# HGRN2 and dilated-window decoder layer with PEER experts: the first half of the tokens multiplied as plain fp32, with whole weight blocks on chip

## The reference, cut to what matters

```python
mod = jax.nn.silu(c) @ w_ada + b_ada                     # 6 x 1024: shifts, scales, gates
n1 = RMSNorm(x) * (1 + sc1) + sh1
h  = n1 @ w_in                                           # 1024 -> 8704: q|f|i|g, q|k|v, two gates
ya = hgrn(h) @ w_branch_a                                # gated linear recurrence, 4 heads of 128
yb = dilated_window_attention(h) @ w_branch_b            # 3 groups of 4 heads; QK norm, partial rotary
x  = x + g1 * ((sigmoid(gl_a) * ya + sigmoid(gl_b) * yb) @ w_out)
n2 = RMSNorm(x) * (1 + sc2) + sh2
q  = rms_norm(n2 @ peer_wq)                              # 8 heads of 256
# top 16 of two times 128 keys, top 16 of their sums, then for each token 128 experts:
x  = x + g2 * sum_k softmax(score)_k * gelu(n2 . u[e_k]) * v[e_k]
```

## Time and profile before

| | us |
|---|---|
| Median of three runs | 4424.8 (4424.0 to 4430.3) |
| Span of the profiled execution | 4435.7 |
| Opening | 0 to 61.4 |
| Projection | 61.4 to 397.3 |
| HGRN | 397.3 to 521.4 |
| Attention, merge | 521.4 to 671.7 |
| Branches | 671.7 to 740.0 |
| Output and second norm | 740.0 to 801.7 |
| Queries, the first gather at 896.3 | 801.7 to 1045.8 |
| Second half beside the experts, and the rest | 1045.8 to 4435.7 |

### The profile page before, as it was taken

How to read it: one execution, slowest core, us unless ns; L and a number is a source line. 1 busy time by engine, 2 the same in 40 slices (tenths; PEclk the granted TensorE clock), 3 DMA queues, 4 the chain that set the end, 5 groups by cost and what they waited for, 6 DMA issues and landing times. The chain is left out here.

```text
span 4435.7 us, 46775 instructions
## 1 busy us (share of the span) xinstructions
PE 3251.9 (73%) x14243; PEld 1706.6 (38%) x14243; DVE 2593.4 (58%) x6557; ACT 1955.8 (44%) x6710; POOL 1472.8 (33%) x1175
## 2 busy tenths in 40 slices
PE   6998868874999999786754687985555555555556
PEld 4677754642543346444432454651111111111111
DVE  2362334476557745584646536656766766766774
ACT  2122431145457734483532225544545545545554
POOL 4543102352322233231212112223444444444443
PEclk8998889986999999787976898987867677777769
DMA  6533244389999999796999978889999999999998
GB/s 258 198 138 129 71 154 171 115 347 356 393 384 356 378 365 387 288 358 232 402 315 383 369 277 308 348 321 383 421 404 421 420 404 415 413 403 414 415 407 334
DMA packets 313374, 1447.75 MB, mean 326 GB/s; under 512 B 42913, under 2 KB 104257, under 8 KB 164770
## 3 DMA queue, kind: packets, MB, share of 16 engines
q0 software_dynamic: 152064, 1107.36, 62.4%
q1 hardware_dynamic: 146690, 330.19, 21.0%
q10 hardware_dynamic: 14368, 7.21, 0.6%
HBM read 1377.25 MB, written 74.57 MB: 327 GB/s over the span
## 5 line engine op out<-in xcount | busy, mean ns | idle before, releaser
L2928 POOL DMA_INDIRECT uv_ring<-in_peer_uv,pick_idx x1024 | 1134.5, 1108 | 2255.1 <-PE expert_acc L3089 1929.2
L3089 PE MATMUL expert_acc<-uv_ring,diag 128*64 128x512 f32 x3968 | 1263.8, 773 | 665.6 <-ACT diag L3059 629.4
L3016 DVE SCALAR_TENSOR_TENSOR uv_ring<-uv_ring,n_pairs 128x1024 f32<-128x1024 f32 x1024 | 1246.5, 1230 | 672.9 <-DMA uv_ring<-in_peer_uv,pick_idx 639.9
L3089 PEld LDWEIGHTS expert_acc<-uv_ring,diag 128*64 128x64 f32 x3968 | 293.8, 163 | 1519.5 <-ACT diag L3059 994.2
L3046 ACT ACTIVATE gelu_cube<-dots_now 128x2 f32<-128x2 f32 x528 | 105.6, 200 | 929.7 <-DVE uv_ring L3016 854.3
L3054 ACT ACTIVATE pick_weight<-gelu_tanh,pick_share 128x1 f32<-128x1 f32 x1056 | 350.8, 379 | 17.6
L3059 ACT ACTIVATE diag<-half_pattern,pick_weight 128x64 f32<-128x64 f32 x1024 | 300.4, 340 | 16.6
L956 PE MATMUL h_acc_q<-in_w_all_q,n_all_q 128*128 128x512 f32 x640 | 286.8, 601 | 0.0
L3049 ACT ACTIVATE gelu_tanh<-gelu_cube,dots_now 128x1 f32<-128x1 f32 x1056 | 253.3, 286 | 16.2
L3051 ACT ACTIVATE pick_share<-dots_now,pick_prob 128x1 f32<-128x1 f32 x1056 | 245.4, 280 | 0.0
L953 PE MATMUL h_acc_q<-n_all_q,in_w_all_q 128*128 128x272 f32 x896 | 218.0, 399 | 10.0 <-DMA in_w_all_q<-in_w_in 10.0
(11 more groups left out here) (457 smaller groups left out, 4784.8 us busy)
## 6 DMA issues: line engine op xcount, KB each, us to landing
in_w_p<-in_w_in SPq DMA_DIRECT2D x34, 1024.0 KB, 7.2
in_w_all_q<-in_w_in SPq DMA_DIRECT2D x17, 2048.0 KB
ada_w<-in_w_ada SPq DMA_DIRECT2D x10, 2048.0 KB, 8.8
uv_ring<-in_peer_uv,pick_idx POOLq DMA_INDIRECT x1024
past_keys_q<-in_past_keys SPq DMA_DIRECT2D x16, 1024.0 KB
past_rows_q<-in_past_values SPq DMA_DIRECT2D x16, 1024.0 KB
score_pair<-scores SPq DMA_DIRECT2D x66, 128.0 KB
wq_raw_p<-in_peer_wq SPq DMA_DIRECT2D x16, 512.0 KB, 5.7
```

Source lines behind the costliest of these rows:

```text
L2928: pool.indirect_dma_start(self.rows_of(part, s), None, self.x["peer_uv"][0], bass.IndirectOffsetOnAxis(ap=self.idx[:, q % 2, s, k:k + 1], ...
L3016: ins = dve.scalar_tensor_tensor(out=row, in0=row, scalar=1.0, in1=self.n2[:, tile % 2, s if tile < LAST_TILE else 0, :], op0=ALU.mult, op ...
L3089: ins = pe.matmul(self.acc[s * 64:(s + 1) * 64, c, :], self.diag[:, part % DIAGS, s, :], rows, start=first, stop=last)
```

## The change

In the first half a product is one plain fp32 matmul where there were three passes. All high and low parts go, with the casts and subtractions on GpSimd and VectorE. `InWeights` has four slots of a whole block, 2 MB each, and asks for a block in one transfer when the block four ahead of it in the slots has been multiplied. Two blocks are asked for in the opening. The last block is asked for behind all units, and the stage doesn't wait for it. `GateBlocks` reads its blocks from the same slots, and its gaps for GpSimd go. `w_out` is loaded whole, `peer_wq` has four slots. `COST` goes from 3.0 to 2.0, `C_Q` likewise, and `MOD_US` from 250 to 310. `TAKEN`, the order of the blocks, is the one that there was. The second half keeps its instructions and their order.

```diff
-    HALF = DC // 2
-
-    def __init__(self, nc, keep, x):
-        self.nc, self.w_dram = nc, x["w_in"]
-        self.raw = keep("in_w_p", [P, 2, DC // 2, BLOCK])
-        self.hi, self.lo = [], []
-        self.grow(keep, 1)
-        sem = lambda name: nc.alloc_semaphore(name=name)
-        self.raw_in = [sem("in_w0_loaded"), sem("in_w1_loaded")]
-        self.split_own, self.split_done = sem("split_own"), sem("split_done")
-        self.order = Order(nc.gpsimd, self.split_own)
+    SLOTS = 4
+    OPENING = 2
+    TAKEN = tuple(range(17))
+
+    def __init__(self, nc, keep, x, slots):
+        self.nc, self.w_dram, self.w = nc, x["w_in"], []
+        self.grow(keep, slots)
+        self.landed = [nc.alloc_semaphore(name=f"in_w{k}_loaded") for k in range(self.SLOTS)]
 
     def grow(self, keep, slots):
-        for k in range(len(self.hi), slots):
-            self.hi.append(keep(f"in_w_hi{k}_p", [P, DC, BLOCK], F32R))
-            self.lo.append(keep(f"in_w_lo{k}_p", [P, DC, BLOCK], F32R))
-
-    def part(self, half):
-        return slice(half * self.HALF, (half + 1) * self.HALF)
+        for k in range(len(self.w), slots):
+            self.w.append(keep(f"in_w{k}_p", [P, DC, BLOCK]))
+
+    def of(self, n):
+        return self.w[n % self.SLOTS]
 
     def load(self, n):
-        sp = self.nc.sync
-        for half in range(2):
-            at_least(sp, self.split_done, 2 * n + half - 1)
-            sp.dma_start(self.raw[:, half], self.w_dram[n][:, self.part(half)]).then_inc(self.raw_in[half], 16)
-
-    def split(self, n, half):
-        pool, b, c = self.nc.gpsimd, n % GateBlocks.SLOTS, self.part(half)
-        pool.wait_ge(self.raw_in[half], 16 * (n + 1))
-        self.order.link(pool.tensor_copy(self.hi[b][:, c], self.raw[:, half]))
-        pool.tensor_tensor(self.lo[b][:, c], self.raw[:, half], self.hi[b][:, c].bitcast(F32), ALU.subtract).then_inc(self.split_done, 1)
+        self.nc.sync.dma_start(self.of(n)[:], self.w_dram[self.TAKEN[n]]).then_inc(self.landed[n % self.SLOTS], 16)
...
+        for n in range(in_weights.OPENING):
+            in_weights.load(n)
...
-        for c in range(DC):
-            dve.wait_ge(moved, c + 1)
-            link(nc.vector.tensor_copy(n_hi[:, c, :], x_t[:, c, :]))
-            nc.vector.tensor_tensor(n_lo[:, c, :], x_t[:, c, :], n_hi[:, c, :].bitcast(F32), ALU.subtract)
...
+        w = self.weights.of(self.before + k)
         if half == 0:
-            at_least(pe, self.split_done, 2 * (k + 1 - self.SPLIT))
+            pe.wait_ge(*self.weights.landed_by(self.before + k))
             at_least(pe, self.staged, t - 1)
         for c in range(half * DC // 2, (half + 1) * DC // 2):
-            for w_part, n_part in ((self.w_lo, self.n_hi), (self.w_hi, self.n_lo), (self.w_hi, self.n_hi)):
-                ins = pe.matmul(self.acc[:, t % 2, :], w_part[b][:, c, m * P:(m + 1) * P], n_part[:, c, :],
-                                start=(c == 0 and w_part is self.w_lo), stop=(c == DC - 1 and w_part is self.w_hi and n_part is self.n_hi))
+            ins = pe.matmul(self.acc[:, t % 2, :], w[:, c, m * P:(m + 1) * P], self.n_all[:, c, :], start=(c == 0), stop=(c == DC - 1))
...
-    COST = 3.0 if span.split else 3.7
+    if alone:
+        assert sorted(InWeights.TAKEN[:len(blocks)]) == list(range(len(blocks)))
+        blocks = [blocks[k] for k in InWeights.TAKEN[:len(blocks)]]
+    COST = 2.0 if alone else 3.7
...
+            at_least(sp, unit_done, first[n - W_SLOTS + 1] if n >= W_SLOTS else 0)
+            if alone:
+                in_weights.load(n)
...
+        for n in range(InWeights.OPENING if alone else 0, W_SLOTS - 1):
+            load(n)
...
-            load(n + (2 if span.split else 1))
+            load(n + W_SLOTS - 1)
...
-        if span.split:
-            load(len(blocks) + 2)
-            for half in range(2):
-                sp.wait_ge(raw_in[half], 16 * LOADED)
+        for n in range(len(blocks) + W_SLOTS - 1, all_blocks):
+            load(n)
...
-                order.link(nc.vector.tensor_copy(mix_hi[:, m, :], part[:, 0, :]))
-                nc.vector.tensor_tensor(mix_lo[:, m, :], part[:, 0, :], mix_hi[:, m, :].bitcast(F32), ALU.subtract).then_inc(mixed, 1)
...
+                ins = pe.matmul(out[:, n % 2, half, :], mix[:, c, n * P:(n + 1) * P], weights.w[:, half, c, :], start=(c == 0), stop=(c == DC - 1))
...
-            order.link(nc.gpsimd.tensor_copy(w_hi[:, s], raw[:, s]))
-            nc.gpsimd.tensor_tensor(w_lo[:, s], raw[:, s], w_hi[:, s].bitcast(F32), ALU.subtract).then_inc(split_done, 1)
...
+                    ins = nc.tensor.matmul(acc[:, v % SLOTS, 0:n], raw[:, u % W_SLOTS, c, :], n_all[:, c, t0:t0 + n], start=(c == 0), stop=(c == DC - 1))
...
-MOD_US = 250.0
+MOD_US = 310.0
```

## The result

The changed kernel takes 4468.3 us (median of 4, 4455.9 to 4476.2) against 4425.5 (median of 4, 4424.0 to 4430.3): a ratio of 1.0095, with a 95% interval of 1.0075 to 1.0114. (The ratios here are worked out from all the runs of both kernels and can differ by 0.1% from the quotient of the medians, which is 1.0097 here.) It is 43 us slower, where 208 us less were forecast; the time lies outside the range. The span of its profiled execution is 4469.8 us, before 4435.7.

A forecast was written before the change was run, and what follows sets the result against it. TensorE was taken to bound the projection, with plain products cheaper than three passes. Gains 9.5 + 129 + 6 + 6 + 10 + 8 + 14 + 25 = 207.5 us, so 4424.8 - 207.5 = 4217 us; range 4188 to 4263.

The forecast's parts named there:

- The price of a step: One 128x512 product over 128 rows, 736 in all: 0.681 us in three passes becomes 0.43 plain, gaining 0.25 us each.
- The modulation: Projection: eight modulation products with their folds, 2.78 us for two, counted as 11 us both before and after.
- Rival (e): Slower: a plain product costs more than three split ones, as at the low clock; 4527 us, chance 0.03.
- the opening: Start of the kernel, to 61.4 us: casts, subtractions and GpSimd stalls go, 9.5 us less (8 to 11).
- the branches: Stage from 671.7 to 740 us: products already plain; a 5.85 us wait and two VectorE operations go, gain 8.
- the gathers without splits between them: Queries beside gathers: splits leave GpSimd's queue, worth about 4 of the 6 us the share leaves; forecast gain 6.
- the rest keeps its time: Everything behind the first half, 1045.8 to 4435.7 us, has the same instructions and keeps its 3390 us.
- the gain of the projection: Projection stage, 61.4 to 397.3 us: 129 us from shorter products and 6 at its end, 135 in all.
- those of the other stages: Gains forecast outside the projection: opening 9.5, HGRN 6, attention and merge 10, branches 8, output 14, queries 25 us.
- The wait at the projection's end: After the last product, 11 us waiting for 2 MB of weights become 5, gain 6 us.
- The signs of being wrong: Projection waits for stores or weights over 10 us, granted clock there below 0.9, or the second half's 3390 us changing.
- Stalls: Projection before the change: TensorE waits 18 us for VectorE's rotations, held up by GpSimd's subtractions; these go.

The follow-up runs named there:

- e4_gpsimd_busy: Changed kernel with 26 casts and subtractions of 128x2048 put back on GpSimd in the projection, on spare tiles nobody reads: 4484.6 us, ratio 1.0108.
- v1_split_act_dve: Kernel before with plain products from the branches on, projection weight parts mostly made by ScalarE and VectorE, no end wait for a gate block's load: 4392.7 us, ratio 0.9930.

## Why the prediction was wrong

- **The price of a step, the term of the sum that failed.** "Eight from 677.42 to 680.86, that is 0.43 us each. That is the price that decides." The eight rows are four products, 0.86 us each. "0.681 becomes 0.43, a gain of 0.25 us a step" should have read 0.681 becomes 0.863, a loss of 0.18. The sign of the whole turned on it.
- **The page of the Trainium skill that I set aside.** "FP8 and Floating Point Precision", section "TensorE Precision Notes", says four passes for true FP32. I worked out 0.91 us from it and wrote that "the trace disagrees". The trace agrees within 5%: 0.863 us is 3.8 of the 0.227 us passes of the earlier trace rows. When a page and a row are apart by a factor of about two, the row is to be counted again before the page is dropped.
- **The modulation.** "Eight modulation products with their folds, 2.78 us for two" has the same slip: x16 and x2 are one turn of eight products and a fold. Eight turns cost 22 us, not 11. With both prices the projection stage nearly closes. Before: 416 x 0.681 + 22 = 305, 2 at the low clock at the start and 2 behind the wait at 296 us, 12 for rotations and low parts together, 1 for an early part: 322 of the 325 to the last product, and 3 stay open. After: 416 x 0.863 + 22 = 381; TensorE is busy for 382.7 us of the stage.
- **Rival (e)** had the right sign and the right point, "above 0.681 us a step", but with the wrong mechanism (the clock) and a chance of 0.03. The clock was 0.99 in the projection; that its 0.86 is also the measured price is chance, for it doubles 0.43 for the clock, and the doubling lay in the rows. Its 4527 put all 736 steps on the path; 416 of them were (76 us); HGRN, attention, output and the first part of the queries together lost 18 us net.
- **Right:** the opening (11.1 for 9.5, VectorE's splits and GpSimd's stalls gone), the branches (8.4 for 8), the gathers without splits between them (8.0 for 6; 141.4 to 142.8 us in the five kernels with plain queries, 149.1 and 149.5 in the two with GpSimd's splits), and that the rest keeps its time. With half the steps the sum held to within 4 us (211 for 207.5), the gain of the projection forecast 8 too high and those of the other stages together some 11 too low. The wait at the projection's end gave 6.2 us for 6.
- **The signs of being wrong** that I named (waits of over 10 us, a clock below 0.9, a changed second half) all stayed away. None of them was the price, which decided the forecast and was taken from one row.
- **The range.** The ends as given for the terms add up to 165 and 235, not 162 and 237; it changes nothing.
- **Stalls:** 18 us for rotations was 12, two engines' rows for the same waits added, and in 7.6 of the 12 a low part was late as well.

The gains around the products, 11.1 + 15 + 6 + 8.4 + 8.0, some 48 us, were real, and the products took them all: 76 us in the projection and those 18, which with the 48 makes the 42 lost, within 4.

## What to carry to other kernels

Before a row's duration becomes a price, set the count of the rows beside the count of the instructions in the code: a plain fp32 matmul is two rows here, an fp32r one a single row. Three fp32r passes of high and low parts (0.681 us for 128x512) beat one plain fp32 product (0.863) wherever TensorE sets the pace; in the stages behind the merge the two forms came out even here, and the plain form saves memory and instructions. What could be saved in the split form was who made the parts: ScalarE and VectorE between units did it without a stall, which gave some 15 us in the projection, and the wait at its end 6 more. These, not the plain product, were the gain to be had.

## What the runs showed of the hardware

- A plain fp32 product of 128x512 over 128 rows costs 0.863 us at the 2.4 GHz level (granted clock 0.99 over the stage), in two rows 0.43 apart; an fp32r product 0.227 us in one.
- A subtraction of 128x2048 on GpSimd (4.60 us) holds up small VectorE operations for up to 4.5 us (TENSOR_TENSOR of 128x64; a TENSOR_SCALAR of 128x4 took 3.83 us); the stall goes with the GpSimd work (longest 227 ns) and comes back with it (median 2.0 us in e4_gpsimd_busy). The same subtraction is 2.29 us on VectorE, and the cast is 1.91 us on ScalarE (L147 in v1_split_act_dve) and 1.90 on GpSimd (L146 before).
- The second half, with the same instructions, took between 3369.8 and 3389.9 us over eight profiled executions; differences of 10 us in the whole time can come from there alone. What makes this scatter no run shows.
